# Expert token rows: picked by matrix products from rows kept in SBUF, in place of a DRAM store, row lists, indirect gathers and transposes

## The chip, the cores and the metric

The kernel runs on one core of one Trainium2 chip, in one launch. The metric is the device time of that launch in microseconds (us), the median of several runs. TensorE is called PE, VectorE DVE, ScalarE ACT, GpSimd POOL and SyncE SP.

## The reference, cut to what matters

A first block (attention with three branches, two layers), then a second one with an even layer (LRU and attention, a dense feed-forward) and an odd one (gated linear attention and a mixture of experts), for 256 tokens of width 1024, all in float32. The change lies in the mixture of experts, which comes last:

```python
D_MODEL, SEQ, N_EXPERTS, TOP_K, D_FF_EXPERT = 1024, 256, 8, 2, 3584

def moe_swiglu(hn, router, w1, w3, w2):
    t = hn.reshape(-1, d)
    logits = (t @ router).astype(jnp.float32)
    top_vals, top_idx = lax.top_k(logits, TOP_K)
    top_w = jax.nn.softmax(top_vals, axis=-1)
    gates = jnp.sum(top_w[..., None] * jax.nn.one_hot(top_idx, N_EXPERTS), axis=1)
    out = jnp.zeros_like(t)
    for e in range(N_EXPERTS):
        h_e = jax.nn.silu(t @ w1[e]) * (t @ w3[e])
        out = out + gates[:, e:e + 1] * (h_e @ w2[e])
    return out

# the last lines of the second block
h = h + moe_swiglu(rms_norm_2(h, norm_ffn[layer]), od_router, od_exp_w1, od_exp_w3, od_exp_w2)
return rms_norm_2(h, norm_final)
```

Each token goes to two of eight experts only, so the kernel gives an expert only the tokens routed to it.

## The kernel before, in words

**Items.** The mixture runs as a chain of items, one expert with up to 128 (a heavy item) or up to 64 tokens (a light item, `ROOM` = 64). In the profiled execution there are eight: light, heavy, heavy, light, heavy, heavy, light, light. The first is `light_item(FIRST, ...)`, the next six come from `KINDS`, written out one after the other, and the last is one turn of a loop whose count the router sets. An expert that overflows its room gets a further light item; here none was needed. In this document the items are counted 1 to 8.

**Weights.** An item needs 42 *halves* (`halves`, `NH`), each a 1 MB tile of 128 x 2048 floats of w1, w3 or w2. They come over SP's DMA queue (line 3437) into a ring of 14 slots in `pool` (`ERING`); the first 20 of the first item are loaded ahead, in six slots of another ring besides. SP issues the load of a half when PE has finished the half that held its slot, 14 earlier: it waits on `item_products`.

**Products.** A heavy item computes in three float32r products per tile (lines 799 to 801): ACT copies each half to `w_hi` (line 2236, six buffers), DVE takes the rest into `expert_lo` (line 3071), PE multiplies. A light item multiplies the raw halves as float32, with 64 stationary columns twice side by side (lines 1585 and 1612). A float32 product that is no transpose is two records in the trace. Within an item PE's order is written out: `up(w, g, ...)` is a product with w1 or w3 for group `g`, `turn_hidden(blk)` transposes the hidden rows into `bank6`, `down(blk)` multiplies by w2. ACT and DVE do the rest of the work of an item behind numbered halves, by the table `BEHIND`: silu, product, high and low part of the hidden columns, the gates, and in the end the input of the next item (`xe`, behind half 41).

**How the next item's tokens are found.** DVE builds `pick_tok` (step `pick`, behind half 20), a 0/1 matrix of tokens by slots. PE multiplies it with the column `token_no` (`list_rows`, line 1441), DVE turns the result into a list of row numbers (line 3260), POOL gathers these rows of 4 KB from `h_rows` in DRAM with one indirect DMA into `xe_tok` (lines 3402 and 3404), and PE transposes them in eight pieces into `bank7` and `bank3` (`turn_gathered`, line 1435), ahead of the item's last two `down`. ACT and DVE take them from there: `xe_hi` and `xe_lo` for a heavy item, `xe_light` for a light one. `h_rows` is written once by POOL (line 3395) from `h_tok`, the normed tokens. Once that store has landed, the room of `h_tok` in SBUF is reused: `hT2` and `hid2`, the second buffers of the hidden rows, lie over it. Only the first item picks its tokens by a product of `h_tok` with `pick_tok` (`gather`, line 1425).

Of the kernel before, what the change touches and what calls it, by code (L numbers as in the profile page):

```python
# [24 lines left out]
F32 = mybir.dt.float32  # L25
# [7 lines left out]
P = 128  # L33
# [10 lines left out]
def shape_constants(S):  # L44
# [33 lines left out]
    token_no = np.stack([np.arange(S).reshape(S // P, P).T, np.ones((P, S // P))], axis=2).reshape(P, -1)  # L78
    out = dict(token_no=token_no, ident=np.eye(P), onehot=onehot, window=window, cos=cos, sin=sin, rot=rot, causal=causal,
# [22 lines left out]
def two_blocks(nc, A, C, out, known):  # L102
# [29 lines left out]
    with ExitStack() as under:  # L132
        sb("below_h_lo", 2 * D, within=under)
        h_lo = sb("h_lo", KD, S, dt=F32R, within=under)
    x = sb("x", KD, S)
# [72 lines left out]
    hT = [(sb("hT_hi", 4, P, dt=F32R), sb("hT_lo", 4, P, dt=F32R))]  # L208
    hid = [sb("hid", BLK)]
    with ExitStack() as under:  # L210
        hT.append(tuple(sb("hT2_" + n, 4, P, dt=F32R, within=under) for n in ("hi", "lo")))
        hid.append(sb("hid2", BLK, within=under))
    h_tok = sb("h_tok", NT, D)
    acc = h.rearrange("p a b -> p (a b)").rearrange("p (t d) -> p t d", t=NT)
    xe_tok = x.rearrange("p a b -> p (a b)")[:, 0:D]
    y_rows = x.rearrange("p a b -> p (a b)")[:, D:2 * D]
    norm_row = pool[:, 2 * EHALF:2 * EHALF + D]
# [136 lines left out]
    token_no, gather_no, row_turn = split(few(2 * NT), NT, 2), few(1), few(1)  # L354
# [40 lines left out]
    h_stored, rows_gathered, rows_taken = sem("h_stored"), sem("rows_gathered"), sem("rows_taken")  # L395
# [245 lines left out]
    def low_slot(q):  # L641
# [4 lines left out]
              25: [("hid", 3), ("hid", 4)], 26: [("rows", 0)], 29: [("hT", 3)], 33: [("hT", 4)], 37: [("hid", 5), ("hid", 6)],  # L646
# [62 lines left out]
    h_rows = nc.dram_tensor("h_rows", (S, D), F32, kind="Internal").ap()  # L709
# [4 lines left out]
    def _(pe):  # L714
# [703 lines left out]
        def gather(turned=None):  # L1418

            for g, n in enumerate((FREE, 0)):  # L1420
                if turned:
                    pe.wait_ge(turned, when(turned, "h", NT - 1, g))
                for c in range(4):
                    for t in range(NT):
                        m = nc.tensor.matmul(bank[n][:, P * c:P * c + ROOM],
                                             h_tok[:, t, P * (4 * g + c):P * (4 * g + c) + P],
                                             pick_tok[:, t, 0:ROOM], start=(t == 0), stop=(t == NT - 1))
                yield g, m

        def turn_gathered():  # L1430

            for g, n in enumerate((FREE, 3)):
                for c in range(4):
                    at_ = P * (4 * g + c)
                    m = nc.tensor.transpose(bank[n][:, P * c:P * c + P], xe_tok[:, at_:at_ + P], ident)
                yield g, m

        def list_rows():

            for t in range(NT):  # L1440
                m = nc.tensor.matmul(bank[FREE][:, 0:2], pick_tok[:, t], token_no[:, t], start=(t == 0), stop=(t == NT - 1))
            return m
# [3 lines left out]
        for g, m in gather(tok_ready):  # L1446
            m.then_inc(psum_ready, wrote("gather", g))
# [22 lines left out]
        def expert_item(i, after_light):  # L1470
# [71 lines left out]
            pe.wait_ge(item_scalar, at(item_scalar, i, "gateT"))  # L1542
            pe.wait_ge(item_vector, at(item_vector, i, "pick"))
            list_rows().then_inc(item_products, tick(item_products, "rows"))
# [21 lines left out]
        def light_item(i, after_light, first=False):  # L1566
# [88 lines left out]
            pe.wait_ge(item_scalar, at(item_scalar, i, "gateT"))  # L1655
            pe.wait_ge(item_vector, at(item_vector, i, "pick"))
            owed.count(list_rows(), "rows")
# [10 lines left out]
            pe.wait_ge(rows_gathered, 16 * (i + 2 + AHEAD))  # L1668
            for g, m in turn_gathered():
                owed.count(m, "gather", g)  # L1670
# [3 lines left out]
        light_item(FIRST, False, first=True)  # L1674
        for i, former, light in zip(NEXT, (True,) + KINDS, KINDS):
            (light_item if light else expert_item)(i, former)
# [3 lines left out]
        with pe.Fori(0, count - 1 - AHEAD) as i:  # L1680
            light_item(i, True)
# [12 lines left out]
    def _(act):  # L1694
# [159 lines left out]
        for l in range(L):  # L1854
# [10 lines left out]
            if l == 0:  # L1865
# [13 lines left out]
                fetch(loaded_tables, token_no.rearrange("p a b -> p (a b)"), C["token_no"])  # L1879
# [433 lines left out]
        def light_item(i, packed, after_light, first=False):  # L2313

            owed = Owed(item_scalar)
            for q in range(NH):
                owed.skip("hi", q)
                for step, n in after(q):
# [56 lines left out]
    def _(dve):  # L2375
# [760 lines left out]
        def item_tables():  # L3136
# [5 lines left out]
            ours = split(y_rows[:, 0:NE * NE], NE, NE)  # L3142
            terms = split(y_rows[:, NE * NE:6 * NE * NE], 5, NE, NE)
            over = split(y_rows[:, 6 * NE * NE:6 * NE * NE + NT * NE], NT, NE)
            held, late = y_rows[:, 512:512 + NE], split(y_rows[:, 520:520 + NT * NE], NT, NE)
            M = MAXI - NE
            excess, shares, before_, until = (y_rows[:, 544 + 8 * n:552 + 8 * n] for n in range(4))
            share = split(y_rows[:, 576:576 + SHARES * NE], SHARES, NE)
            mine, reached = (split(y_rows[:, 600 + M * NE * n:600 + M * NE * (n + 1)], M, NE) for n in range(2))
            part = split(y_rows[:, 680:680 + M * NT * NE], M, NT, NE)  # L3150
            number = split(y_rows[:, 760:760 + M * NE], M, NE)
# [104 lines left out]
        def list_of_rows(i):  # L3256

            dve.wait_ge(rows_taken, i + 2 + AHEAD)
            dve.wait_ge(item_products, at(item_products, i, "rows"))
            return V.tensor_scalar(gather_no.bitcast(I32), bank[7][:, 0:1], float(S - 1), None, ALU.min)  # L3260

# [10 lines left out]
        def expert_item(i, packed=False):  # L3272
            for q, (w, blk, half) in enumerate(halves):
                expert_lower(i, q)
                for step, n in after(q):
# [6 lines left out]
                    elif step == "hT":  # L3282
                        dve.wait_ge(item_scalar, at(item_scalar, i, "hT", n))
                        hT_hi, hT_lo = hT[n % 2]
                        V.tensor_tensor(hT_lo, split(bank[6], 4, P), hT_hi.bitcast(F32), ALU.subtract)\
                            .then_inc(item_vector, tick(item_vector, "hT", n))
                    elif step == "gateT":
                        slots_used(i).then_inc(item_vector, tick(item_vector, "slots"))
                    elif step == "pick":
                        pick_rows(i, packed).then_inc(item_vector, tick(item_vector, "pick"))  # L3290
                    elif step == "rows":
                        list_of_rows(i).then_inc(item_vector, tick(item_vector, "rows"))
                    elif step == "xe" and n == (0 if packed else 1):
                        low_gathered(i, n, packed).then_inc(item_vector, tick(item_vector, "xe"))
                    elif step == "xe" and not packed:
                        low_gathered(i, n, packed)

        def light_item(i, packed, first=False):

            owed = Owed(item_vector)  # L3300
            for q in range(NH):
# [3 lines left out]
                for step, n in after(q):  # L3305
# [19 lines left out]
                    elif step == "rows":  # L3325
                        owed.count(list_of_rows(i), "rows")
# [27 lines left out]
    def _(pool_engine):  # L3354
# [36 lines left out]

        for t in range(NT):
            for g in range(2):
                pool_engine.wait_ge(tok_ready, when(tok_ready, "h", t, g))
            pool_engine.dma_start(h_rows[P * t:P * t + P, :], h_tok[:, t])\
                .then_inc(h_stored, tick(h_stored, "all", by=16))
        pool_engine.wait_ge(h_stored, when(h_stored, "all"))
        G.tensor_tensor(row_turn, eps, eps, ALU.add).then_inc(rows_taken)

        def gather_rows(i, light):  # L3400
            pool_engine.wait_ge(item_vector, at(item_vector, i, "rows", items=-AHEAD))
            G.tensor_tensor(row_turn, eps, eps, ALU.add).then_inc(rows_taken)
            few_ = slice(0, ROOM if light else P)
# [3 lines left out]
        for t in range(NT):  # L3407
            for g in range(2):
                pool_engine.wait_ge(tok_ready, when(tok_ready, "x", t, g))
        for i, light in zip(range(-1, AHEAD), KINDS + (True,)):  # L3410
            gather_rows(i, light)
        pool_engine.wait_ge(route_ready, when(route_ready, "items"))
        count = pool_engine.value_load(item_count[0:1, 0:1].bitcast(I32), min_val=NE, max_val=MAXI)
        with pool_engine.Fori(AHEAD, count - 1) as i:
            gather_rows(i, True)
# [111 lines left out]
```

## Time and profile before

| what | us |
|---|---|
| median of 3 runs (1992.86 to 2000.18) | 1995.07 |
| the profiled execution: its time | 1998.74 |
| its span in the trace | 1996.3 |
| PE busy | 1927.9 (97%) |
| DVE busy | 1230.2 (62%) |
| ACT busy | 945.5 (47%) |
| POOL busy | 53.1 (3%) |

The mixture of experts fills the span from about 1130 us on. "Busy" of PE counts a matmul from its start to its modelled end, and matmuls overlap, so the distance between starts is what one costs in a row of them. The chain of waits is the work that ended last, followed back from the end. A window is a stretch in us from the span's start.

### The profile page before, as it was taken

The numbers are of one execution on the slowest core, as the hardware profiler recorded it, in microseconds if no ns is written. First come the engines' busy times: TensorE is split into PE (matmuls) and PEld (weight loads), VectorE is DVE, ScalarE is ACT, GpSimd is POOL, SyncE is SP. The second block draws the span as 40 slices with busy tenths as digits, with TensorE's granted clock in tenths as the row PEclk, the third lists the DMA queues.
The fourth block names the chain that finished last, engine by engine and source line by source line (L and its number), as shares of the span: only waits on it lengthen the run. The fifth ranks groups of instructions, "written<-read, shape, count | busy, mean of one in ns | idle before, by whom it ended". The sixth has DMA issues, their size and how long they took to land.

```text
span 1996.3 us, 30473 instructions
## 1 busy us (share of the span) xinstructions
PE 1927.9 (97%) x12208; PEld 1583.4 (79%) x12208; DVE 1230.2 (62%) x1803; ACT 945.5 (47%) x1372; POOL 53.1 (3%) x38
## 2 busy tenths in 40 slices
PE   5999999999999999999999999999998999999876
PEld 5899999999999998999999836888843788883321
DVE  7656986666886676666654217988811988961001
ACT  2645563555563475434463206777611866750001
POOL 0000000000000030000000000100000010000000
PEclk7999999999999999999999999999999999999999
DMA  9977365565643542655364999999999999999997
GB/s 300 241 230 220 111 191 149 111 183 156 190 119 121 180 148 94 202 181 179 113 211 181 345 409 404 409 404 381 376 392 404 409 408 405 397 363 402 404 404 317
DMA packets 313405, 541.08 MB, mean 271 GB/s; under 512 B 68029, under 2 KB 208241, under 8 KB 313273
## 3 DMA queue, kind: packets, MB, share of 16 engines
q1 hardware_dynamic: 306384, 530.81, 75.4%
q10 hardware_dynamic: 5704, 4.19, 0.7%
q0 software_dynamic: 1184, 4.19, 0.6%
q8 instruction: 97, 1.59, 0.3%
q14 instruction: 36, 0.29, 0.0%
HBM read 537.04 MB, written 2.12 MB: 270 GB/s over the span
## 4 chain that ended last, share of the span: by engine, by line
PE 84%; DMA 7%; DVE 3%; SPq 3%; ACT 1%; issue 1%; ACTq 0%; DVEq 0%
PE bank L799 20%; PE bank L801 20%; PE bank L800 20%; PE bank L1585 6%; DMA pool<-in_od_exp_w 6%; SPq L3437 3%; PE bank L746 3%; PE bank L1612 2%; PE bank L952 1%; PE bank L1381 1%; PE bank L759 1%; PE bank L1467 1%; DMA ring<-in_w_in 1%; PE bank L935 1%; PE bank L925 1%
## 5 line engine op out<-in xcount | busy, mean ns | idle before, releaser
L3071 DVE TENSOR_TENSOR expert_lo<-pool,w_hi 128x2048 fp32r<-128x2048 f32 x168 | 376.4, 2286 | 48.0 <-ACT w_hi L2236 47.9
L2236 ACT ACTIVATE w_hi<-pool 128x2048 fp32r<-128x2048 f32 x168 | 311.8, 1912 | 22.1 <-DMA pool<-in_od_exp_w 19.2
L799 PE MATMUL bank<-h_upper,upper 128*128 128x256 f32 x1056 | 311.7, 295 | 3.9 <-DVE h_lo L2595 3.2
L800 PE MATMUL bank<-h_lo,upper 128*128 128x256 f32 x1056 | 299.2, 283 | 0.0
L801 PE MATMUL bank<-h_upper,ring_lo 128*128 128x256 f32 x1056 | 299.2, 283 | 0.0
L2496 DVE TENSOR_TENSOR ring_lo<-ring,upper 128x1024 fp32r<-128x1024 f32 x148 | 180.0, 1222 | 103.7 <-ACT upper L1752 103.2
L799 PEld LDWEIGHTS bank<-h_upper,upper 128*128 128x128 f32 x1056 | 202.6, 192 | 6.7 <-issue 5.0
L1585 PE MATMUL bank<-pool,xe_light 128*64 128x512 f32 (+1 forms) x976 | 192.0, 541 | 14.5 <-DMA pool<-in_od_exp_w 14.5
L800 PEld LDWEIGHTS bank<-h_lo,upper 128*128 128x128 f32 x1056 | 202.8, 192 | 1.7 <-issue 0.2
L801 PEld LDWEIGHTS bank<-h_upper,ring_lo 128*128 128x128 f32 x1056 | 202.6, 192 | 0.0
L2795 DVE TENSOR_TENSOR piece_lo<-ring,piece_hi 128x1024 fp32r<-128x1024 f32 x118 | 144.7, 1236 | 73.8 <-ACT piece_hi L1741 73.5
L799 PE MATMUL bank<-w_hi,xe_hi 128*128 128x512 f32 x448 | 178.6, 399 | 5.1 <-DVE expert_lo L3071 5.1
L801 PE MATMUL bank<-w_hi,xe_lo 128*128 128x512 f32 x448 | 175.2, 391 | 0.0
L800 PE MATMUL bank<-expert_lo,xe_hi 128*128 128x512 f32 x448 | 174.9, 390 | 0.0
L1752 ACT ACTIVATE upper<-ring 128x1024 fp32r<-128x1024 f32 x148 | 155.1, 1054 | 38.2 <-DMA ring<-in_w_in 21.0
L1585 PEld LDWEIGHTS bank<-pool,xe_light 128*64 128x64 f32 x976 | 66.1, 137 | 128.8 <-issue 85.5
L3315 DVE TENSOR_TENSOR hid<-hid,bank 128x512 f32<-128x512 f32 (+1 forms) x16 | 9.9, 621 | 237.7 <-PE bank L1585 237.7
L1741 ACT ACTIVATE piece_hi<-ring 128x1024 fp32r<-128x1024 f32 x118 | 123.2, 1053 | 51.4 <-PE bank L801 51.3
L1612 PE MATMUL bank<-pool,hT_light 128*64 128x512 f32 x448 | 103.5, 598 | 10.3 <-DMA pool<-in_od_exp_w 10.1
L799 PEld LDWEIGHTS bank<-w_hi,xe_hi 128*128 128x128 f32 x448 | 84.5, 189 | 25.4 <-DVE expert_lo L3071 7.2
L2339 ACT ACTIVATE hT_light<-bank 128x512 f32<-128x512 f32 (+1 forms) x16 | 8.7, 544 | 201.7 <-PE bank L1598 201.7
L799 PE MATMUL bank<-row_hi,piece_hi 128*128 128x256 f32 x352 | 99.9, 284 | 0.0
(464 smaller groups left out, 3858.4 us busy)
## 6 DMA issues: line engine op xcount, KB each, us to landing
pool<-in_od_exp_w SPq DMA_DIRECT2D x330, 1024.0 KB, 14.8
ring<-in_w_in SPq DMA_DIRECT2D x48, 1024.0 KB, 5.4
ring<-in_ev_ffn_w SPq DMA_DIRECT2D x33, 1024.0 KB, 5.4
ring<-in_w_ada SPq DMA_DIRECT2D x24, 1024.0 KB, 6.7
ring<-in_od_w_in SPq DMA_DIRECT2D x12, 1024.0 KB, 5.7
ring<-in_ev_w_in SPq DMA_DIRECT2D x10, 1024.0 KB, 5.3
ring<-in_w_in SPq DMA_DIRECT2D x32, 256.0 KB, 4.6
ring<-in_w_out SPq DMA_DIRECT2D x8, 1024.0 KB, 5.1
```

What stands on the lines that cost most here:

```text
L746: m = nc.tensor.matmul(b[base:base + rows, 0:cols], left(k), right(k), start=(k == 0), stop=(k == K - 1))
L799: nc.tensor.matmul(b, left[0], right[0], start=first, stop=False, skip_group_check=True)
L800: nc.tensor.matmul(b, left[0], right[1], start=False, stop=False, skip_group_check=True)
L801: return nc.tensor.matmul(b, left[1], right[0], start=False, stop=last, skip_group_check=True)
L1585: m = nc.tensor.matmul(b[ROOM * j:ROOM * j + ROOM, 0:cols_], xe_light[:, c], t[:, k, cols_ * j:cols_ * j + cols_], start=c == 0, stop=c == ...
L1612: m = nc.tensor.matmul(bank[Y[0]][ROOM * n:ROOM * n + ROOM], t[:, e, ROOM * j:ROOM * j + ROOM], w[:, k, 512 * n:512 * n + 512], start=blk ...
L1741: nc.scalar.activation(piece_tiles(n, *src.shape[1:])[0], src, ACT.Copy)\
L1752: nc.scalar.activation(upper_tile(n), upper_source(n)[0], ACT.Copy)\
L2236: nc.scalar.activation(w_hi[q % HIS], ring_slot(q), ACT.Copy)\
L2496: V.tensor_tensor(dst, src, upper_tile(n).bitcast(F32), ALU.subtract)\
L2795: V.tensor_tensor(lo, src, hi.bitcast(F32), ALU.subtract).then_inc(piece_ready, tick(piece_ready, n))
L3071: V.tensor_tensor(low_slot(q), ring_slot(q), w_hi[q % HIS].bitcast(F32), ALU.subtract)\
```

## The change

- POOL no longer stores `h_tok` to DRAM and gathers no rows. `h_rows`, `xe_tok`, `token_no`, `gather_no`, `row_turn` and three semaphores go, with PE's `list_rows`, DVE's `list_of_rows` and ACT's one wait for the store.
- In every item PE's `turn_gathered` becomes `gather`: 16 float32 products of `h_tok` (stationary, 128 x 128) with `pick_tok` (64 moving columns where the next item is light, 128 where it is heavy), in the same place and into the same banks.
- `h_tok` has to stay. The second hidden buffers move: `hT2` to the bottom of SBUF, over the first half of `x` (where `xe_tok` was), `hid2` onto the first 512 columns of `y_rows`, the second half of `x`. The router's small tables move to the first half of `x`.

```diff
+    with ExitStack() as under:
+        hT_second = [sb("hT2_" + n, 4, P, dt=F32R, within=under) for n in ("hi", "lo")]
     x = sb("x", KD, S)
 ...
-    hT = [(sb("hT_hi", 4, P, dt=F32R), sb("hT_lo", 4, P, dt=F32R))]
+    hT = [(sb("hT_hi", 4, P, dt=F32R), sb("hT_lo", 4, P, dt=F32R)), hT_second]
     hid = [sb("hid", BLK)]
-    with ExitStack() as under:
-        hT.append(tuple(sb("hT2_" + n, 4, P, dt=F32R, within=under) for n in ("hi", "lo")))
-        hid.append(sb("hid2", BLK, within=under))
     h_tok = sb("h_tok", NT, D)
-    xe_tok = x.rearrange("p a b -> p (a b)")[:, 0:D]
+    table_room = x.rearrange("p a b -> p (a b)")[:, 0:D]
     y_rows = x.rearrange("p a b -> p (a b)")[:, D:2 * D]
+    hid.append(y_rows[:, 0:BLK])
 ...
-        def gather(turned=None):
+        def gather(packed, banks, turned=None):
-            for g, n in enumerate((FREE, 0)):
+            few_ = ROOM if packed else P
+            for g, n in enumerate(banks):
 ...
                 for c in range(4):
                     for t in range(NT):
-                        m = nc.tensor.matmul(bank[n][:, P * c:P * c + ROOM],
+                        m = nc.tensor.matmul(bank[n][:, P * c:P * c + few_],
                                              h_tok[:, t, P * (4 * g + c):P * (4 * g + c) + P],
-                                             pick_tok[:, t, 0:ROOM], start=(t == 0), stop=(t == NT - 1))
+                                             pick_tok[:, t, 0:few_], start=(t == 0), stop=(t == NT - 1))
                 yield g, m
 ...
             up(3, 2, 2, 3)
-            pe.wait_ge(item_scalar, at(item_scalar, i, "gateT"))
-            pe.wait_ge(item_vector, at(item_vector, i, "pick"))
-            list_rows().then_inc(item_products, tick(item_products, "rows"))
             down(1)
 ...
             turn_hidden(6)
-            pe.wait_ge(rows_gathered, 16 * (i + 2 + AHEAD))
-            for g, m in turn_gathered():
+            pe.wait_ge(item_scalar, at(item_scalar, i, "gateT"))
+            pe.wait_ge(item_vector, at(item_vector, i, "pick"))
+            for g, m in gather(packed, (FREE, 3)):
                 m.then_inc(item_products, tick(item_products, "gather", g))
             down(5)
             down(6)
 ...
-                        if first and n == 1:
-                            act.wait_ge(h_stored, when(h_stored, "all"))
 ...
-            pool_engine.dma_start(h_rows[P * t:P * t + P, :], h_tok[:, t])\
-                .then_inc(h_stored, tick(h_stored, "all", by=16))
 ...
-            G.indirect_dma_start(xe_tok[few_], None, h_rows, bass.IndirectOffsetOnAxis(gather_no[few_].bitcast(U32), 0))\
-                .then_inc(rows_gathered, 16)
```

In the order of instructions the change shows on PE at two places. The first is in item 1, a light one, where the group with blocks 3 and 4 has been computed; `small` is `token_no`, `rstd` is `pick_tok`, and `L1585`, `L1612` of before are lines 1566 and 1593 of the changed kernel. Before:

```order
L1585 MATMUL bank3<-pool,xe_light 64x512 [waits expert_loaded1]
L1585 MATMUL bank3<-pool,xe_light 64x512 x3
L1441 MATMUL bank7<-small,rstd 128x2 [waits item_vector,item_scalar]
L1441 MATMUL bank7<-small,rstd 128x2
L1612 MATMUL bank4<-pool,hT_light1 64x512 [waits expert_loaded2,item_scalar]
```

The same place of the changed kernel:

```order
L1566 MATMUL bank3<-pool,xe_light 64x512 [waits expert_loaded1]
L1566 MATMUL bank3<-pool,xe_light 64x512 x3
L1593 MATMUL bank4<-pool,hT_light1 64x512 [waits expert_loaded2,item_scalar]
L1593 MATMUL bank4<-pool,hT_light1 64x512 x3
L1593 MATMUL bank4<-pool,hT_light1 64x512 [waits expert_loaded3]
```

The two products of the list and their wait are gone from here.

The second place is the end of item 2, the first heavy one, between `down(4)` and `down(5)`; the next item is heavy too. Before:

```order
L799 MATMUL bank5<-w_hi1,hT_hi 128x512
L800 MATMUL bank5<-expert_lo11,hT_hi 128x512
L801 MATMUL bank5<-w_hi1,hT_lo 128x512
L1499 MATMUL bank6<-ident,hid 128x128 [waits item_vector]
L1499 MATMUL bank6<-ident,hid 128x128 x3
L1435 MATMUL bank7<-ident,x 128x128 [waits rows_gathered]
L1435 MATMUL bank7<-ident,x 128x128 x3
L1435 MATMUL bank3<-ident,x 128x128 x4
L799 MATMUL bank4<-w_hi2,hT2_hi 128x512 [waits item_vector]
L800 MATMUL bank4<-expert_lo12,hT2_hi 128x512
```

Now, with lines 795 to 797 for 799 to 801 and 1482 for 1499:

```order
L795 MATMUL bank5<-w_hi1,hT_hi 128x512
L796 MATMUL bank5<-expert_lo11,hT_hi 128x512
L797 MATMUL bank5<-w_hi1,hT_lo 128x512
L1482 MATMUL bank6<-ident,hid 128x128 [waits item_vector]
L1482 MATMUL bank6<-ident,hid 128x128 x3
L1422 MATMUL bank7<-rstd,h_tok 128x128 [waits item_vector,item_scalar]
L1422 MATMUL bank7<-rstd,h_tok 128x128 x7
L1422 MATMUL bank3<-rstd,h_tok 128x128 x8
L795 MATMUL bank4<-w_hi2,hT2_hi 128x512 [waits item_vector]
L796 MATMUL bank4<-expert_lo12,hT2_hi 128x512
```

Eight transposes became sixteen products, and the wait for POOL's gather became the waits that `list_rows` had. PE's other rows stand in the same order as before; on ACT one wait is gone, on DVE one instruction of each item, on SP nothing moved.

## Rows read from the trace of the kernel before

**Rows 1.** The page: engines, and the chain that ended last by engine.

```profile
PE 1927.9 (97%) x12208; PEld 1583.4 (79%) x12208; DVE 1230.2 (62%) x1803; ACT 945.5 (47%) x1372; POOL 53.1 (3%) x38
...
PE 84%; DMA 7%; DVE 3%; SPq 3%; ACT 1%; issue 1%; ACTq 0%; DVEq 0%
```

**Rows 2.** Windows: PE, PEld, DVE, ACT, POOL busy, PE clock, DMA share, GB/s.

```profile
1136.00:1213.00 77.00, 77.00 (x396) 28.73 (x396) 17.21 (x89) 13.74 (x20) 1.41 (x3) 1.00 1.02 396
1213.00:1336.00 123.00, 123.00 (x561) 99.89 (x558) 109.58 (x70) 89.59 (x63) 5.02 (x2) 1.00 1.03 407
...
1546.00:1668.00 122.00, 122.00 (x549) 99.42 (x550) 109.72 (x70) 90.80 (x64) 5.01 (x2) 0.99 1.03 407
```

**Rows 3.** Windows: where the DMA rate falls, and the light stretches behind them.

```profile
1360.00:1460.00 100.00, 100.00 (x468) 82.03 (x469) 78.00 (x52) 63.53 (x48) 4.95 (x2) 1.00 1.00 371
1740.00:1800.00 60.00, 60.00 (x308) 47.90 (x307) 37.86 (x23) 29.82 (x24) 4.70 (x2) 1.00 1.00 365
...
1500.00:1546.00 46.00, 40.05 (x191) 13.77 (x187) 5.02 (x6) 6.51 (x7) 1.15 (x2) 0.99 1.03 404
1800.00:1846.00 46.00, 46.00 (x211) 15.78 (x211) 5.21 (x12) 3.14 (x7) 1.09 (x2) 1.00 1.03 403
```

**Rows 4.** The chain in order of time: start, us, what.

```profile
1175.93 0.54 PE bank L1441 x4
...
1205.56 1.02 PE bank L1435 x8
...
1277.88 0.34 PE bank L1441 x4
...
1323.80 0.87 PE bank L1435 x8
...
1346.47 1.72 PE bank L1467 x4
```

**Rows 5.** Timeline of PE: start, us, line, operands, count; a pick of item 1.

```profile
1130.69 3.76 PE L1425 MATMUL bank<-rstd,h_tok 128*128 128x64 f32 x32 [0.28 <-DVE rstd L3125]
1134.29 1.92 PE L1451 MATMUL bank<-ident,x 128*128 128x128 f32 x16
```

**Rows 6.** Timeline of PE: float32 products with 128 moving columns, in the linear attention.

```profile
1054.40 1.06 PE L1295 MATMUL bank<-pool 128*128 128x128 f32 x8
1055.29 0.39 PE L1315 MATMUL bank<-pool 128*128 128x128 f32 x2
```

**Rows 7.** Timelines at the end of item 1: PE, ACT, DVE.

```profile
1206.52 7.09 PE L1612 MATMUL bank<-pool,hT_light 128*64 128x512 f32 x32
...
1206.25 1.09 ACT L2283 ACTIVATE xe_hi<-bank 128x512 fp32r<-128x512 f32 x2 [3.58 <-PE bank L1435]
...
1209.16 8.90 DVE L3071 TENSOR_TENSOR expert_lo<-pool,w_hi 128x2048 fp32r<-128x2048 f32 x4 [0.99 <-ACT w_hi L2236]
```

**Rows 8.** POOL's queue: the whole span, 1500 to 1546, 1800 to 1990 us.

```profile
q0 software_dynamic: 1184, 4.19, 0.6%
...
q0 software_dynamic: 144, 0.52, 2.9%
...
q0 software_dynamic: 160, 0.52, 1.0%
```

**Rows 9.** Timeline of PE: the end of item 4, and of item 8.

```profile
1531.44 1.09 PE L1435 MATMUL bank<-ident,x 128*128 128x128 f32 x8
...
1545.94 0.76 PE L799 MATMUL bank<-w_hi,xe_hi 128*128 128x512 f32 x1 [5.13 <-DVE expert_lo L3071]
...
1975.28 1.09 PE L1435 MATMUL bank<-ident,x 128*128 128x128 f32 x8
1976.30 1.94 PE L1612 MATMUL bank<-pool,hT_light 128*64 128x512 f32 x8
...
1983.58 1.94 PE L1612 MATMUL bank<-pool,hT_light 128*64 128x512 f32 x8 [0.47 <-DMA pool<-in_od_exp_w]
```

More of the change, by code:

```diff
@@ L77, in shape_constants @@
     iota = np.tile(np.arange(P)[None, :], (P, 1))
-    token_no = np.stack([np.arange(S).reshape(S // P, P).T, np.ones((P, S // P))], axis=2).reshape(P, -1)
-    out = dict(token_no=token_no, ident=np.eye(P), onehot=onehot, window=window, cos=cos, sin=sin, rot=rot, causal=causal,
+    out = dict(ident=np.eye(P), onehot=onehot, window=window, cos=cos, sin=sin, rot=rot, causal=causal,
                chunkmask=chunkmask, restart=restart, pick=pick, before=before,
@@ L353, in two_blocks @@
     ssum = few(2)
-    token_no, gather_no, row_turn = split(few(2 * NT), NT, 2), few(1), few(1)
     expert_pos, expert_gate = split(few(NT * NE), NT, NE), split(few(NT * NE), NT, NE)
@@ L394, in two_blocks @@
     pos_ready = sem("pos_ready")
-    h_stored, rows_gathered, rows_taken = sem("h_stored"), sem("rows_gathered"), sem("rows_taken")
     item_products, item_scalar, item_vector = sem("item_products"), sem("item_scalar"), sem("item_vector")
@@ L645, in two_blocks @@
               15: [("hid", 1), ("hid", 2)], 17: [("hT", 1)], 20: [("pick", 0)], 21: [("hT", 2)],
-              25: [("hid", 3), ("hid", 4)], 26: [("rows", 0)], 29: [("hT", 3)], 33: [("hT", 4)], 37: [("hid", 5), ("hid", 6)],
+              25: [("hid", 3), ("hid", 4)], 29: [("hT", 3)], 33: [("hT", 4)], 37: [("hid", 5), ("hid", 6)],
               38: [("hT", 5)], 40: [("hT", 6)], 41: [("xe", 0), ("xe", 1)]}
@@ L708, in two_blocks @@
     scratch = nc.dram_tensor("scratch", (12, 512), F32, kind="Internal").ap()
-    h_rows = nc.dram_tensor("h_rows", (S, D), F32, kind="Internal").ap()
     block = ctx.enter_context(nc.Block())
@@ L1424, in gather @@
                     for t in range(NT):
-                        m = nc.tensor.matmul(bank[n][:, P * c:P * c + ROOM],
+                        m = nc.tensor.matmul(bank[n][:, P * c:P * c + few_],
                                              h_tok[:, t, P * (4 * g + c):P * (4 * g + c) + P],
-                                             pick_tok[:, t, 0:ROOM], start=(t == 0), stop=(t == NT - 1))
+                                             pick_tok[:, t, 0:few_], start=(t == 0), stop=(t == NT - 1))
                 yield g, m
[L1430 to L1442, printed above, removed]
         wait_banks(FREE, 0)
         pe.wait_ge(route_ready, when(route_ready, "picked"))
-        for g, m in gather(tok_ready):
+        for g, m in gather(True, (FREE, 0), tok_ready):
             m.then_inc(psum_ready, wrote("gather", g))
@@ L1468, in sum_rows, with expert_item @@
             count_product(m, "sum", t)
-        def expert_item(i, after_light):
+        def expert_item(i, packed, after_light):
             def count_product(m, *step):
@@ L1564, in expert_item, with light_item @@
             down(6)
-        def light_item(i, after_light, first=False):
+        def light_item(i, packed, after_light, first=False):
             owed = Owed(item_products)
@@ L1654, in light_item @@
             up(3, 2, 0, 1, 2, 3)
-            pe.wait_ge(item_scalar, at(item_scalar, i, "gateT"))
-            pe.wait_ge(item_vector, at(item_vector, i, "pick"))
-            owed.count(list_rows(), "rows")
             down(1)
@@ L1667, in light_item @@
             turn_hidden(6)
-            pe.wait_ge(rows_gathered, 16 * (i + 2 + AHEAD))
-            for g, m in turn_gathered():
+            pe.wait_ge(item_scalar, at(item_scalar, i, "gateT"))
+            pe.wait_ge(item_vector, at(item_vector, i, "pick"))
+            for g, m in gather(packed, (FREE, 3)):
                 owed.count(m, "gather", g)
@@ L1672, in light_item @@
             down(6)
-        light_item(FIRST, False, first=True)
-        for i, former, light in zip(NEXT, (True,) + KINDS, KINDS):
-            (light_item if light else expert_item)(i, former)
+        light_item(FIRST, KINDS[0], False, first=True)
+        for i, former, light, packed in zip(NEXT, (True,) + KINDS, KINDS, KINDS[1:] + (True,)):
+            (light_item if light else expert_item)(i, packed, former)
         pe.wait_ge(route_ready, when(route_ready, "items"))
@@ L1680, in _ @@
         with pe.Fori(0, count - 1 - AHEAD) as i:
-            light_item(i, True)
+            light_item(i, True, True)
         ticks.counts[("item_products", "end")] = ticks.counts["item_products"]
@@ L1878, in _ @@
                 fetch(loaded_tables, iota8, C["iota"][:, 0:8])
-                fetch(loaded_tables, token_no.rearrange("p a b -> p (a b)"), C["token_no"])
                 fetch(loaded_tables, flip, C["flip"])
@@ L3141, in item_tables @@
             square = [P, NE, NE]
[L3142 to L3145, printed above, removed]
+            ours = split(table_room[:, 0:NE * NE], NE, NE)
+            terms = split(table_room[:, NE * NE:6 * NE * NE], 5, NE, NE)
+            over = split(table_room[:, 6 * NE * NE:6 * NE * NE + NT * NE], NT, NE)
+            held, late = table_room[:, 512:512 + NE], split(table_room[:, 520:520 + NT * NE], NT, NE)
             M = MAXI - NE
[L3147 to L3151, printed above, removed]
+            excess, shares, before_, until = (table_room[:, 544 + 8 * n:552 + 8 * n] for n in range(4))
+            share = split(table_room[:, 576:576 + SHARES * NE], SHARES, NE)
+            mine, reached = (split(table_room[:, 600 + M * NE * n:600 + M * NE * (n + 1)], M, NE) for n in range(2))
+            part = split(table_room[:, 680:680 + M * NT * NE], M, NT, NE)
+            number = split(table_room[:, 760:760 + M * NE], M, NE)
             for n, light in enumerate((True,) + KINDS + (True,)):
@@ L3254, in pick_rows @@
             return m
[L3256 to L3260, printed above, removed]
         def low_gathered(i, n, packed):
@@ L3290, in expert_item @@
                         pick_rows(i, packed).then_inc(item_vector, tick(item_vector, "pick"))
-                    elif step == "rows":
-                        list_of_rows(i).then_inc(item_vector, tick(item_vector, "rows"))
                     elif step == "xe" and n == (0 if packed else 1):
@@ L3324, in light_item @@
                         owed.count(pick_rows(i, packed), "pick")
-                    elif step == "rows":
-                        owed.count(list_of_rows(i), "rows")
                     elif step == "xe" and n == (0 if packed else 1):
@@ L3390, in _ @@
                 pool_engine.wait_ge(clog_rows, ticks.counts["clog_rows"])
-        for t in range(NT):
-            for g in range(2):
-                pool_engine.wait_ge(tok_ready, when(tok_ready, "h", t, g))
-            pool_engine.dma_start(h_rows[P * t:P * t + P, :], h_tok[:, t])\
-                .then_inc(h_stored, tick(h_stored, "all", by=16))
[L3397 to L3403, printed above, removed]
-            G.indirect_dma_start(xe_tok[few_], None, h_rows, bass.IndirectOffsetOnAxis(gather_no[few_].bitcast(U32), 0))\
-                .then_inc(rows_gathered, 16)
[L3407 to L3415, printed above, removed]
     @block.sync
```

## The prediction

> **What bounds the kernel now.** I began with the page's engines and its chain [rows 1]: PE is busy 97% of the span and is 84% of the chain, DMA 7%. An average says little here, so I cut the expert stage into its items with the windows [rows 2]. In items 1, 2 and 5 PE is busy all of the time, and at once the DMA engines move 396 to 407 GB/s. Both seem to be the limit, so the question is which of them waits for the other. The windows answer that [rows 3]: late in each pair of heavy items the rate falls to 371 and 365 GB/s while PE stays at 100%. There all 14 slots are taken, and a load can start only when PE frees one; PE is the limit, and the fourteen slots are a full store. Behind each pair comes light work, in which PE needs a half about every 1.8 us (7.09 us for 4 halves [rows 7]) and the DMA brings one about every 2.6 us (1.05 MB at 404 GB/s): the rate is back at 404 and 403 [rows 3], the store runs down, and in the end PE waits for landings [rows 9].
>
> So the end is built like this: PE's time through items 1 to 3, then the DMA's time for what item 4 and the start of item 5 need beyond the full store, then PE's time through items 5 and 6, then the DMA's time to the last half, which starts at 1983.58 us [rows 9]. PE time added in items 1, 2, 3, 5, 6 moves the end by all of it, since the loads behind it can't start before PE frees slots. PE time added in items 4, 7 and 8 lies beside the DMA. DMA bytes removed count only in the other stretches, about 1500 to 1546 us and 1800 us to the end.
>
> **What a pick costs PE.** The new `gather` is 16 products, 32 records. With 64 columns the trace has it already, in item 1: the 32 records start at 1130.69 and the next work at 1134.29 [rows 5], so 3.60 us, 0.112 each. With 128 columns there is no such pick. The nearest rows are the eight records of line 1295, of the same shape, which take from 1054.40 to 1055.29 [rows 6]: 0.89 us, 0.111 each, and 3.56 for 32. The time is no longer for 128 columns than for 64, so it is not the moving side that sets it. From below it can't be under what 64 columns take; from above, if load and stream of a record don't overlap, the stream comes on top. Line 1467 streams 512 columns in 1.72 / 4 = 0.43 us [rows 4], so 128 columns in 0.107, and a record would take 0.11 + 0.107 = 0.22, a pick 7.0. I take 3.56, since those rows have the same shape.
>
> The Trainium skill (TensorE: Matmul & The Clock Gate, section "The mechanism" and "LDWEIGHTS (loading the stationary operand)") has a rule that speaks against the change: a weight load overlaps a running matmul only if the two use other row groups, and 128 weight columns take about 107 ns; all records here use all rows, so by it each 128-column record is load plus stream. This case's rows speak against the rule, since 64 and 128 columns take the same; what it would give is the second rival below.
>
> **What goes.** In a heavy item the eight transposes (0.87) and the list (0.34); in item 1 they are 1.02 and 0.54 [rows 4]. No wait goes with them: PE never waits for the gathered rows, as the chain shows the transposes right behind other PE work.
>
> **The sum on PE, where it counts:**
> - item 1 (next is heavy): 3.56 - 1.02 - 0.54 = +2.0
> - items 2 and 5 (next is heavy): 3.56 - 0.87 - 0.34 = +2.35 each
> - items 3 and 6 (next is light): 3.60 - 1.21 = +2.4 each
>
> Together +11.5 us.
>
> **Where it is hidden.** In item 4 the pick begins at about 1531 [rows 9] and makes PE 2.5 us later (the list no longer helps, since PE then waits for landings); PE stood idle 5.13 us before item 5, waiting for the first half of item 5 to land and to be split. If that cover were gone, it would cost 2.5. Item 7 is the same with half a microsecond of wait at each of the following halves. Item 8 is the last: the pick starts at 1975.28, ends 3.6 later at 1978.9, three more halves of 1.76 bring the start of the last to 1984.2, where it was 1983.58 [rows 9]. That is +0.6, and the cover ends there. (This last pick serves no item, as before.)
>
> **ACT and DVE at the change of items.** In item 1 the transposed rows are there at 1206.5, PE then has 7 us of products to 1213.5, and the first low part is done at 1209.16 + 2.2 = 1211.4 [rows 7]. So there are 2.1 us of slack after 4.9 us of work; counted from the end of the pick this stays as it is, since the pick keeps its place ahead of the same two `down`. In the heavy items PE has 10 us of products behind the pick. I cost it at nothing.
>
> **DMA.** The store and the eight gathers are 4.19 MB [rows 8], 10.4 us at 404 GB/s if all of it were on the path. On the path are the gather of item 4 (0.52 MB between 1500 and 1546) and those of items 7 and 8 (0.52 MB from 1800 on) [rows 8]: 1.3 us each time, -2.6 in all. The rest falls where PE is the limit, and only fills the slots sooner.
>
> **The rest.** DVE's list of rows, POOL's work, ACT's wait for the store and the small table `token_no` lie on nothing that is waited for: DVE is busy 110 of 123 us in a heavy item [rows 2], and loses 0.15 us. The moved buffers keep their shapes, engines and order; `hid2` on `y_rows` is written behind the sum that reads `y_rows`, by waits that were there. Nothing, or up to 1 us either way.
>
> Sum: +11.5 + 0.6 - 2.6 = **+9.5 us**. On the profiled execution, 1998.74 us for a span of 1996.3, that is 2008.2. That execution is 3.7 above the median of the runs shown, 1995.07, and it is the median that I predict from: **2004.5 us**, 0.47% slower. About 0.5%, 10 us, is what a measurement of this kernel can tell from no change, and the forecast lies just inside it.
>
> **Rivals.**
> 1. *DMA is the limit of the whole stage* (faster). If the loads never waited for slots, all 4.19 MB would go from the path and PE's added time would be covered: 1995.1 - 10.4 = 1984.7. For it: over 396 GB/s in almost every window. Against: 371 and 365 GB/s with PE at 100% [rows 3]. It would decide if PE's heavy items took under 42 x 2.6 = 109 us; they take 122. 4%.
> 2. *Load and stream don't overlap at 128 columns.* Three picks that count (items 1, 2, 5) cost 3.4 more each: +10, 2014.7. Against: rows 6. 8%.
> 3. *Most of PE's time is hidden*, because the full store is short-lived and PE's lateness is made good by DMA time saved in the saturated first part. Only one pair's picks count: 1995 to 2000. For it: the rate is low for only some 100 and 60 us. 18%.
> 4. *ACT and DVE become late behind a pick*, because the first half of the pick is now ready 1.3 us later, and item 2 or 5 starts late by 1 to 2 us each, some 4 in all: 2008.5. For it: the slack after item 1 is only 2.1 us. 10%.
>
> The forecast itself has 60%, with 2001 to 2008 as its own range. Taking in the third, the fourth and, in part, the second, the range is 1996 to 2012. Slower by over 0.5% (beyond 2005.05): 40% of the forecast's 60, most of the fourth, all of the second, together 0.40. Faster by over 0.5%: the first rival, 0.04. The rest, 0.56, is no change that can be told.
>
> **What the profile will show.** Right: 32 records of the pick in each item, 3.6 us from the first start to the next work for 64 and for 128 columns alike; items 2, 3, 5 and 6 longer by 2.3 us each between the same lines; the rate still falling late in each pair; PE's idle time ahead of item 5 shorter, near 2 to 4 us; no POOL queue. Wrong: records 0.2 us apart at 128 columns (second rival), no stretch with a lower rate and PE waiting for landings in heavy items (first), waits of PE for `expert_lo` at the start of items 2, 3 or 6 (fourth). The forecast as a whole falls if the end of item 6 comes less than 6 or more than 14 us later, counted from the start of item 1.

## The result, and the profile after

| | before | after |
|---|---|---|
| median of 9 runs each, us | 1998.49 (1992.86 to 2000.18) | 2004.04 (2001.16 to 2006.68) |
| ratio, 95% interval | | 1.0025 (1.0017 to 1.0033) |
| the profiled execution, time and span | 1998.74, 1996.3 | 2004.04, 2002.1 |

The changed kernel is slower by 0.25%, 5.0 us (3.4 to 6.6 by the interval). The forecast was 9.5 us slower: right in direction, nearly double in size. The first three runs of before (median 1995.07) were low against the later ones, so the forecast time of 2004.5 hits the measured 2004.04 partly by that luck; the difference is what the forecast has to be judged by.

The page of the changed kernel, engines and the chain by engine, against [rows 1]:

```profile
PE 1944.0 (97%) x12368; PEld 1604.1 (80%) x12368; DVE 1230.7 (61%) x1795; ACT 946.3 (47%) x1372; POOL 27.0 (1%) x19
...
PE 88%; DMA 5%; DVE 2%; SPq 2%; ACT 1%; issue 1%; ACTq 0%; DVEq 0%
```

PE is busy 16 us longer; more of the chain is PE and less DMA. The new picks, from the same chain in order of time (start, us, what). The three picks are those of items 1, 2 and 3, against the transposes in [rows 4]:

```profile
1204.43 3.77 PE bank L1422 x32
...
1324.91 3.57 PE bank L1422 x32
...
1449.83 3.52 PE bank L1422 x32
```

The second is one of 128 columns, the third one of 64: both 3.5 to 3.6 us, as the forecast had taken from rows of another stage. The first, also of 128 columns, took 3.77; the light products behind it start 0.2 us after its last record, those of item 2 0.03.

To see where the time went I use the first sum of an item (line 1467 before, 1450 after) as a mark. Chain of the kernel before, the marks in items 4, 5 and 7 (the timeline of PE has each 0.07 us earlier):

```profile
1465.38 1.91 PE bank L1467 x4
...
1558.45 1.06 PE bank L1467 x4
...
1799.12 1.91 PE bank L1467 x4
```

Chain of the changed kernel, the same marks:

```profile
1471.38 1.91 PE bank L1450 x4
...
1563.36 1.06 PE bank L1450 x4
...
1808.42 1.91 PE bank L1450 x4
```

And the last products, before and after, in the timeline of PE (start, us, instruction, idle time ahead and what ended it):

```profile
1986.30 1.99 PE L1689 MATMUL bank<-x,slots 64*128 64x512 f32 x8 [0.79 <-ACT x L2363]
```

```profile
1992.04 1.99 PE L1668 MATMUL bank<-x,slots 64*128 64x512 f32 x8 [0.79 <-ACT x L2339]
```

A stretch here is the time between two such points. With the first pick as the start (1130.69 before [rows 5], 1130.24 after):

| stretch | limit | before | after | change | forecast |
|---|---|---|---|---|---|
| pick of item 1 to the mark in item 4 | PE | 334.69 | 341.14 | +6.45 | +6.75 |
| to the mark in item 5 | DMA | 93.07 | 91.98 | -1.1 | -1.3 |
| to the mark in item 7 | PE | 240.67 | 245.06 | +4.4 | +4.75 |
| to the last products | DMA | 187.18 | 183.62 | **-3.6** | **-0.7** |

The two PE stretches came as forecast, the last one did not. Up to the mark in item 7 the changed kernel is 9.75 us later, with 10.2 forecast and 6 to 14 named as the bounds. The windows tell the same for the limits (columns as in [rows 2]); of the changed kernel, answering to the first two lines of [rows 3]:

```profile
1360.00:1460.00 100.00, 100.00 (x469) 82.67 (x469) 80.78 (x53) 62.27 (x46) 0.00 (x0) 1.00 0.95 352
1740.00:1800.00 60.00, 60.00 (x290) 50.28 (x289) 43.27 (x26) 33.79 (x25) 0.00 (x0) 1.00 0.95 352
```

The rate falls further than before, to 352 GB/s from 371 and 365, with PE at 100%: the slots are full, and PE is the limit. Ahead of item 5 PE's idle time shrank, from 5.13 [rows 9] to 2.97 us (timeline of the changed kernel):

```profile
1536.76 3.84 PE L1422 MATMUL bank<-rstd,h_tok 128*128 128x128 f32 x32
1540.53 7.09 PE L1593 MATMUL bank<-pool,hT_light 128*64 128x512 f32 x32
1550.59 0.47 PE L795 MATMUL bank<-w_hi,xe_hi 128*128 128x512 f32 x1 [2.97 <-DVE expert_lo L3047]
```

So the pick of item 4 was hidden, as forecast. The last pick was not. Same timeline, the end of item 8:

```profile
1978.58 1.94 PE L1593 MATMUL bank<-pool,hT_light 128*64 128x512 f32 x8 [0.53 <-DMA pool<-in_od_exp_w]
1980.45 3.79 PE L1422 MATMUL bank<-rstd,h_tok 128*128 128x64 f32 x32
1984.16 7.09 PE L1593 MATMUL bank<-pool,hT_light 128*64 128x512 f32 x32
```

Behind the pick PE runs its last four halves without a wait, where it had waited for each of the last three before. The landings in the traces give what that costs: the last half landed at 1988.70 and PE took it up at 1989.36, against 1983.53 and 1983.58 before. So the last pick keeps PE 0.6 us behind, as forecast.

### The profile page after: what moved, and what is told of

Same layout as the page of the kernel before. It is cut to its first block, busy times and chain, and to the rows that moved or that the text cites. A ratio compares the mean times of both kernels' runs of the same rounds, so it can differ in the third digit from the quotient of the medians.

```text
span 2002.1 us, 30744 instructions
## 1 busy us (share of the span) xinstructions
PE 1944.0 (97%) x12368; PEld 1604.1 (80%) x12368; DVE 1230.7 (61%) x1795; ACT 946.3 (47%) x1372; POOL 27.0 (1%) x19
## 4 chain that ended last, share of the span: by engine, by line
PE 88%; DMA 5%; DVE 2%; SPq 2%; ACT 1%; issue 1%; ACTq 0%; DVEq 0%
PE bank L795 21%; PE bank L797 20%; PE bank L796 20%; PE bank L1566 7%; DMA pool<-in_od_exp_w 4%; PE bank L1593 3%; PE bank L742 3%; SPq L3378 2%; PE bank L948 2%; PE bank L1422 1%; PE bank L1377 1%; PE bank L755 1%; PE bank L1450 1%; PE bank L931 1%; PE bank L917 1%
## 5 line engine op out<-in xcount | busy, mean ns | idle before, releaser
L1566 PE MATMUL bank<-pool,xe_light 128*64 128x512 f32 (+1 forms) x976 | 191.7, 541 | 12.6 <-DMA pool<-in_od_exp_w 12.5
L797 PE MATMUL bank<-row_hi,piece_lo 128*128 128x256 f32 x352 | 99.6, 283 | 0.0
```

The source lines that it names most:

```text
L797: return nc.tensor.matmul(b, left[1], right[0], start=False, stop=last, skip_group_check=True)
L1566: m = nc.tensor.matmul(b[ROOM * j:ROOM * j + ROOM, 0:cols_], xe_light[:, c], t[:, k, cols_ * j:cols_ * j + cols_], start=c == 0, stop=c == ...
```

## The experiments

**Theory.** PE's added time counts in full in items 1 to 3, 5 and 6. The last stretch lost more than the bytes of two gathers because a gather of 64 rows slows the loads beyond its bytes. **Rivals.** The gather costs its bytes only, and a fuller store of slots gave the rest; the moved buffers gave it; or lateness of PE in a heavy pair is made good by the DMA later. All ratios are to the kernel before on the same chip; differences in us are the ratio times its median there.

What points at the gather is the DMA view of the kernel before in windows of 20 us. Between 1830 and 1850 us the rate, in slices of 0.5 us, is

```profile
GB/s 401 401 426 442 401 401 401 401 401 401 434 434 401 401 410 393 401 410 426 426 410 393 410 238 262 262 254 369 426 401 410 401 401 410 418 426 401 410 410 401
...
q0 software_dynamic: 80, 0.26, 4.8%
```

For about 2 us, some 5 us after POOL issued the 64-row gather, the total rate, gather included, is 238 to 262. Between 1500 and 1520, around the gather of 128 rows in item 4, no slice falls under 377:

```profile
GB/s 410 401 418 426 410 401 401 402 418 401 426 418 410 401 401 410 410 401 434 401 418 401 393 418 410 402 426 418 410 401 393 410 418 401 426 418 410 426 377 393
...
q0 software_dynamic: 144, 0.52, 6.6%
```

So the 64-row gather, at half the bytes, costs (409 - 255) / 409 x 2 = 0.75 us besides its 0.65, 1.4 in all (an estimate, from the mean rate of 409 in the 20 us before).

The DMA view also tells how the rate falls. Queues, packets, MB and share of the 16 engines' time, in 2 us within the 64-row gather (1841 to 1843), then in 2 us within the 128-row one (1507.5 to 1509.5):

```profile
q1 hardware_dynamic: 87, 0.32, 58.4%
q0 software_dynamic: 73, 0.26, 47.8%
...
q0 software_dynamic: 102, 0.42, 52.4%
q1 hardware_dynamic: 103, 0.41, 51.1%
```

The engines are taken up in full in both, but finish 160 packets in the one and 205 in the other. Around the gather of 128 rows a packet of 4 KB takes 159 to 172 ns, 164 in the mean. Around that of 64 it takes up to 338, in the mean 230 for the weights' packets and 237 for the rows'. At one time up to 13 packets of the 64-row gather are under way (12 of the other), of 16 to 20 in all, so it is not carried by half of the engines. It writes partitions 0 to 63 only, the other one all 128; whether that is why each packet takes longer, no run here tells.

**Without gathers.**

```diff
-            G.indirect_dma_start(xe_tok[few_], None, h_rows, bass.IndirectOffsetOnAxis(gather_no[few_].bitcast(U32), 0))\
-                .then_inc(rows_gathered, 16)
+            G.tensor_tensor(row_left, eps, eps, ALU.add).then_inc(rows_gathered, 16)
```

> The kernel before with all eight indirect gathers left out (POOL counts them as done; the experts get stale rows), the store, the lists and the transposes kept. What a gather costs the DMA engines where they are the limit, after item 3 and after item 6. Theory (a gather of 64 rows slows all loads for about 2 us and costs 1.4 us, as much as one of 128 rows): 1.35 in item 4 and 2 x 1.4 in items 7 and 8, so 4.2 us faster than before, and the stretch from the start of item 7 to the end about 2.8 us shorter than the 193.5 us of before. Rival (a gather costs its bytes, 0.65 us for 64 rows; the rest of what the changed kernel won back in its last items came from a fuller store of slots): 2.6 us faster, the last stretch 1.3 us shorter. PE's busy time the same by both.

Measured: 0.998 (0.9968 to 0.9993), 4.0 us faster, with an interval (1.4 to 6.4) that holds both numbers. The trace is sharper. Mark of item 7 and last products, timeline of PE:

```profile
1801.10 1.98 PE L1467 MATMUL bank<-x,slots 128*128 128x512 f32 x4
...
1983.98 1.99 PE L1689 MATMUL bank<-x,slots 64*128 64x512 f32 x8 [0.79 <-ACT x L2363]
```

The last stretch is 182.88 against 187.2, the stretch of item 4 91.1 against 93.1; PE's stretches are the same to 0.1 us. What the changed kernel won in its last stretch (3.6, and 0.6 more that its last pick took) is won here by leaving out the gathers, with PE untouched.

**Silu buffer and router's tables moved, nothing else.**

```diff
-        hid.append(sb("hid2", BLK, within=under))
+    hid.append(y_rows[:, 0:BLK])
-            ours = split(y_rows[:, 0:NE * NE], NE, NE)
+            ours = split(xe_tok[:, 0:NE * NE], NE, NE)
...
```

> The kernel before with one part of the change: the second silu buffer lies on the first half of the rows y, and the router's small tables on the first half of x. Store, lists, gathers and transposes stay. Theory: nothing, within 0.1% of before. Rival (moved buffers gave the changed kernel part of the 3.5 us that the forecast missed): 2 to 3 us faster.

Measured: 1.0002 (0.9993 to 1.0011). The moved silu buffer and tables give nothing that can be told: at most 1.4 us faster by the interval, and the rival asked for 2 to 3. The move of `hT2` was not run by itself; in the changed kernel PE's stretches came as forecast with it. The last stretch here was 185.6 us, though, 1.6 under that of the first trace of before: one trace of a stretch in which the DMA is the limit is good to some 2 us only.

**Gathers of 128 rows for light items.**

```diff
-            few_ = slice(0, ROOM if light else P)
+            few_ = slice(0, P)
```

> The kernel before, with 128 rows instead of 64 in the gathers for light items (items 3, 6, 7, 8 issue them). Theory (64 rows cost what 128 rows do, because they occupy only some of the DMA engines for as long): no change, within 1 us, and no dip of the rate to 240 to 290 GB/s at about 1838 and 1936 us. Rival (cost by bytes): 2 x 0.65, 1.3 us slower.

Measured: 0.9996 (0.9987 to 1.0006), 0.8 us faster, from 2.6 faster to 1.2 slower. Twice the bytes cost nothing more that can be told; the rival's 1.3 lies just outside. The dip is gone at the same place and time, between 1830 and 1850 us:

```profile
GB/s 410 410 401 410 410 426 410 393 418 410 401 410 410 434 401 393 418 410 401 410 418 426 401 401 410 410 401 402 418 426 410 401 410 410 401 410 418 418 410 393
```

Nor is there one in item 8, where the lowest slice between 1925 and 1945 is 393 too. The last stretch is 184.9 us. The expectation's reason, that 64 rows occupy only some of the engines, does not hold, by the packets under way above.

**Five gathers in place of one,** in items 7 and 8, of 64 and of 128 rows:

```diff
+            spare = [w_hi[n].bitcast(F32)[:, D * half:D * half + D] for n in range(2) for half in range(2)]
-            G.indirect_dma_start(xe_tok[few_], None, h_rows, ...)
+            for dst in [xe_tok] + spare * more:
+                G.indirect_dma_start(dst[few_], None, h_rows, ...)
 ...
```

PE's wait counts the further gathers. For 128 rows `few_` is 128 wide in items 7 and 8, so that their own two gathers grow as well.

> The kernel before; the gathers that items 7 and 8 issue (64 rows each) are done five times, the further four into buffers that light items don't use, and PE waits for all. Eight more gathers where the DMA is the limit. Theory (each slows the loads for 2 us and costs 1.4 to 1.5 us): 11 to 12 us slower than before. Rival (0.65 us each, by bytes): 5.2 us slower.

> As the kernel with the five gathers of 64 rows, but 128 rows each in items 7 and 8. By bytes a gather of 128 rows costs 1.3 us, without a dip of the rate: 10 to 11 us slower than before by both theories. With the theory (64 rows cost as much as 128) it comes out within 1.5 us of the 64-row kernel, by the rival 5 us slower than that.

Measured: 1.0063 (1.0044 to 1.0083), 12.6 us slower (8.8 to 16.6), for 64 rows, and 1.0036 (1.0024 to 1.0048), 7.2 us slower (4.8 to 9.6), for 128. The theory holds for 64 rows (1.6 us each), and the rival's 5.2 lies outside. For 128 rows the expectation of 10 to 11 was a miss: half the bytes cost more, not the same. The two intervals overlap a little, but of the eleven runs with 128 rows only one (2008.77) is above the lowest of the five with 64 (2007.77). In the traces the last stretch is 197.0 and 195.4 us, against 185.6 and 187.2, so 1.3 and 1.1 for each of the eight; they show only about 1.7 of the 5.4 us between the two kernels. Windows over the five gathers, of the kernel with 64 rows:

```profile
1828.00:1838.00 10.00, 10.00 (x50) 3.46 (x46) 0.32 (x1) 0.60 (x1) 0.00 (x0) 1.00 1.03 409
1838.00:1848.00 10.00, 10.00 (x49) 3.54 (x50) 0.43 (x2) 0.60 (x1) 4.66 (x6) 1.00 1.03 341
1848.00:1858.00 10.00, 9.60 (x46) 2.93 (x42) 0.00 (x0) 0.60 (x1) 0.00 (x0) 1.00 1.02 318
```

and of the kernel with 128:

```profile
1838.00:1848.00 10.00, 10.00 (x50) 3.49 (x48) 0.00 (x0) 0.60 (x1) 4.71 (x5) 1.00 1.03 410
1848.00:1858.00 10.00, 9.40 (x44) 2.93 (x42) 0.00 (x0) 0.60 (x1) 0.00 (x0) 1.00 1.02 409
```

The DMA engines are shown busy all the time in both (shares 1.02 and 1.03), yet they move 318 to 341 GB/s with 64 rows and 409 to 410 with 128.

**Picks done twice,** in items 5 and 6, in items 2 and 3, and in items 4 and 7 of the changed kernel:

```diff
-                for c in range(4):
+                for c in [c for _ in range(times) for c in range(4)]:
-            for g, m in gather(packed, (FREE, 3)):
+            for g, m in gather(packed, (FREE, 3), times=2 if isinstance(i, int) and i in (-3, -2) else 1):
```

> The changed kernel with the pick done twice in items 5 and 6 (the second overwrites the first with the same values): 7.1 us more on PE, in the second pair of heavy items. Theory (PE is the limit there, its time moves the end by nearly all, less about 0.6 us for loads that land meanwhile): +5 +6.5 to 7.1, 11.5 to 12.1 us slower than before. Rival (PE lateness in the pair is made good by the DMA in the last two items): +5 to +8.

> The changed kernel with the pick done twice in items 2 and 3, 7.1 us more on PE in the first pair. Theory: as above, 11.5 to 12.1 us slower than before. Rival: made good in item 4, +5 to +8.

> The changed kernel with the pick done twice in items 4 and 7, the light ones behind a pair or within the last loads: 7.1 us more on PE where the DMA is the limit. Theory: hidden but for what goes over the 3.0 us that PE stands idle ahead of item 5: 0 to 1 us above the changed kernel, so +5 to +6 on before. Rival (PE is the limit everywhere, light items too): +12.

Measured: 1.0052 (1.0031 to 1.0073), 10.4 us; 1.0056 (1.0037 to 1.0075), 11.2 us; 1.0025 (1.0013 to 1.0036), 5.0 us. The same 7.1 us of PE time costs 5.4 and 6.2 beyond the changed kernel behind either pair of heavy items, and nothing in items 4 and 7. The intervals are 4 us to either side; their low ends, 6.2 and 7.4, lie under the rival's upper end of 8, so the timing alone doesn't exclude that PE's lateness is partly made good. The traces do. With the picks doubled in items 5 and 6, the marks in items 5 and 7 and the last products (timeline of PE) are

```profile
1562.46 1.13 PE L1450 MATMUL bank<-x,slots 64*128 64x512 f32 x4
...
1814.67 1.55 PE L1450 MATMUL bank<-x,slots 128*128 128x512 f32 x3
...
1997.99 1.56 PE L1668 MATMUL bank<-x,slots 64*128 64x512 f32 x6 [0.79 <-ACT x L2339]
```

and with them doubled in items 2 and 3, the marks in items 4 and 5 are

```profile
1477.53 1.98 PE L1450 MATMUL bank<-x,slots 128*128 128x512 f32 x4
...
1567.02 1.13 PE L1450 MATMUL bank<-x,slots 64*128 64x512 f32 x4
```

| stretch | changed kernel, twice traced | doubled in 5 and 6 | doubled in 2 and 3 | doubled in 4 and 7 |
|---|---|---|---|---|
| pick of item 1 to the mark in item 4 | 341.1, 341.1 | 341.1 | **348.2** | 341.1 |
| to the mark in item 5 | 92.0, 91.1 | 89.9 | 89.5 | 90.9 |
| to the mark in item 7 | 245.1, 245.1 | **252.2** | 245.1 | 245.1 |
| to the last products | 183.7, 183.4 | 183.3 | 183.2 | 183.4 |

A doubled pair adds 7.1 us to its own stretch. The stretch behind it, where the rival would have the lateness made good, is no shorter than those of the other kernels by more than 0.4 us (89.5 against 89.9, and 183.3 against 183.2 to 183.7). Doubling in items 4 and 7 adds nothing to any stretch; the rival asked for 12 us.

**The pick of light items earlier.**

```diff
             up(3, 3, 0, 1, 2, 3)
+            if not first:
+                pe.wait_ge(item_scalar, at(item_scalar, i, "gateT"))
+                pe.wait_ge(item_vector, at(item_vector, i, "pick"))
+                for g, m in gather(packed, (FREE, 3)):
+                    pass
             down(3)
```

> The changed kernel with the pick of items 4, 7 and 8 moved ahead of down(3), where PE waits for landings anyway. Theory (the pick of the last item, late behind its loads, costs 0.6 us at the end; elsewhere it is hidden): 0.6 us faster than the changed kernel, so +4.5 to +5 on before. Rival (the last pick is hidden too, the end is set by the last landing alone): the same as the changed kernel.

Measured: 1.0036 (1.0023 to 1.0049), not faster than the changed kernel in timing. In its trace PE waits for the last landing again, as before (timeline):

```profile
1983.86 1.94 PE L1593 MATMUL bank<-pool,hT_light 128*64 128x512 f32 x8 [0.48 <-DMA pool<-in_od_exp_w]
```

and the last stretch is 182.9 us, against 183.7 and 183.4 in the two traces of the changed kernel. PE takes up the last half at 1983.86, having landed at 1983.82; in the changed kernel 0.66 us lie between the two, in both traces. The wait is moved off the end as meant, and what it gives, 0.6 us, is under what the timing can show.

**The changed kernel again.**

> The changed kernel once more, on the same chip as the two others: +4 to +7 us on before. In its trace the stretches where PE is the limit repeat to 0.1 us; those where the DMA is the limit may differ by 1 to 2 us from the first trace.

Measured: 1.0025 (1.0013 to 1.0037), 5.0 us slower, the same. PE's stretches repeat to 0.1 us. The stretch of item 4 took 91.1 us, after 92.0 in the first trace.

No version that computes the same was faster than the kernel before beyond the noise. One that gathers the rows in heavy items, where the DMA has time to spare, and picks them by products in light ones, where PE has, was not run.

## Why the prediction was right, and where its size was off

- *The limits stage by stage*: right. PE's added time went to the end in full in its own stretches (+10.85 of 11.5 forecast), and nothing of the picks in items 4 and 7 did. The doubled picks showed both, by the stretches of their traces.
- *What a pick costs*: right, 3.57 us for 128 columns and 3.52 for 64 in the chain, 3.49 for both from the first start to the next work in items 2 and 3. The second rival (records 0.2 us apart) is out. Item 1 became 2.06 us longer (forecast 2.0), each of the heavy items 2.2 (forecast 2.35 and 2.4); that is the 0.65 us missing of 11.5. The list had cost more than its own 0.34 us. In the kernel before, the first two products behind it start 0.32 us apart, where such products otherwise start 0.23 apart (timeline of PE, item 2):

```profile
1277.49 0.39 PE L801 MATMUL bank<-w_hi,xe_lo 128*128 128x512 f32 x1
1277.71 0.50 PE L1441 MATMUL bank<-small,rstd 128*128 128x2 f32 x4
1278.08 0.49 PE L799 MATMUL bank<-w_hi,hT_hi 128*128 128x512 f32 x1
1278.40 0.40 PE L800 MATMUL bank<-expert_lo,hT_hi 128*128 128x512 f32 x1
```

- *The last pick*: right, 0.6 us, shown by the landings in the traces only.
- *ACT and DVE at the change of items*: right, no wait in items 2, 3 and 6.
- *DMA*: this term of the sum was mis-sized. It was -2.6, by bytes, 1.3 for item 4 and 1.3 for items 7 and 8. The last stretch alone fell by 3.6 with a pick of +0.6 in it, so it won 4.2 in the first pair of traces. Between the trace without the gathers (182.9) and those with them (187.2 and 185.6) lie 4.3 and 2.7. Two gathers at 1.4 us, bytes and dip together, are 2.8 of it; that a 64-row gather costs well over its 0.65 us of bytes is shown by the experiment with five. In item 4, where the gather has 128 rows and no dip, seven traces without it took 89.5 to 92.0 us and five with it 92.7 to 93.5: about 2.5, with 1.3 for the bytes. What the rest of that is stays open; the same code in item 4 differed by 2 us between traces, so the number of slots filled at the start of item 4 may well not be the same each time.
- *The third rival* (most is hidden) is the one that the timing resembles, but its reason is refuted: PE's time wasn't hidden, the DMA gave more back. With +10.85 on PE, +0.6 for the last pick and -5.3 for the three gathers in the first pair of traces (1.1 in item 4, 4.2 in the last stretch), the sum is 6.15, within the measured 3.4 to 6.6. By the means of all traces (without the last pick's 0.6) the gathers are 2.5 and 3.6, and the sum is 5.35.
- *The base*: the forecast set out from a median of three, 1995.07; nine gave 1998.49. In twelve traces the pick of item 1, ahead of which the kernels differ only in a small table, in where buffers lie and in the store of `h_tok` (issued at 1129.6 in the kernel before), begins between 1127.67 and 1134.71 us. That scatter is larger than the effect, and only many runs on the same chip bring out 5 us.

## What to carry to other kernels

Where two engines alternate as the limit, sum a change by stretch: the same 7 us of matrix products were free in the light items and moved the end of a heavy pair by 7 us, 5 to 6 of which the timing of the whole showed. Look for the stretches in the DMA rate, not in busy shares: PE was at 100% in both, but the rate fell where PE was the limit. And price a transfer that is taken off a saturated queue from the fall of the total rate around it, not from its bytes alone.

## What the runs showed of the hardware

- An indirect gather of 64 rows of 4 KB into 64 partitions cut the total DMA rate to 238 to 262 GB/s for 2 us; one of 128 rows, twice the bytes, left it at 377 or more. Five in a row moved 318 to 341 GB/s with 64 rows and 409 to 410 with 128. Over the whole kernel eight more of them cost 12.6 us with 64 rows and 7.2 with 128.
- Around the 64-row gather 4 KB packets took longer, 230 to 237 ns in the mean against 164, with the engines shown busy all the time. A loss of this kind doesn't show in the DMA's busy share, only in the GB/s.
- A float32 product with a 128 x 128 stationary operand took 0.110 to 0.113 us per record with 64 moving columns and 0.112 to 0.115 with 128, two records each (picks of the changed kernel).
